# Taking a layer's experts in an order computed on the chip: most groups and fewest groups in turn

## The chip, the cores and the metric

One core of one Trainium2 chip runs one inference step of a two-layer network, all in float32. The metric is the time on the device in microseconds (us), lower is better. Three runs of the kernel before took 1150.02, 1155.69 and 1157.26 us.

## What is computed

There are 384 tokens of width 1024 (128 of the prompt, 256 of the sample). Layer 0 mixes tokens by a long convolution, layer 1 by attention; after each comes a mixture of experts, which is what the change touches:

```
g_sel  = argmax(t @ w_group + b_group)                 # one of 4 groups of experts
e_prob = softmax(of the 4 experts of that group)
top_w, top_i = top_k(e_prob, 2)                        # two experts of the 16 for each token
combine = sum over the two of one_hot(expert) * g_w * top_w
for e in range(16):
    a, b = split(t @ w_up[e], 2)
    y += combine[:, e] * ((silu(a) * b) @ w_down[e])
x = layer_norm(alpha * x + gate * y)
```

Each expert has 6 MB of weights: `w_up[e]` is 1024 x 1024 and `w_down[e]` 512 x 1024, float32. The sum over experts has no order of its own.

## The kernel before

**Groups.** The kernel computes an expert only for the tokens that chose it. A token's row is copied into one or two *slots*; an expert owns a whole number of groups of 32 slots (`SLOT_TOK`), at least one, and slots of expert 0 come first, then those of expert 1, and so on. With the inputs used there are 33 groups in each layer. For a group TensorE does three things in `expert(e, nb, base)`: 32 matmuls with the two up pieces, 12 matmuls that add the group before to the result (`combine`), 16 matmuls with the down piece. After an expert's last group a tiny matmul of the identity counts up `expert_done`.

**Weights.** They come in pieces of 2 MB, three to an expert: 48 pieces to a layer, numbered i = 3 * expert + c, c = 0 and 1 up, 2 down. The ring has 11 places (`RING + EXTRA`), so piece i goes where piece i - 11 was. SyncE (SP) issues the pieces in order, in `experts(l)`: an up place is free when `up_ready` has counted the last group of the expert that held it, a down place when `expert_done` has. Pieces 0 to 10 have conditions of their own, among them: piece 8 waits until VectorE has added `row_beta` to the last token tile (`ln_done`), piece 9 until the token rows have been written to their slots (`slots_filled`) and TensorE has gathered groups 0 to 2, piece 10 for `x_added`.

**Routing.** VectorE works out, in a chain of small operations in `moe(l)`, the groups of each expert (`nbase[:, 0:16]`), their running sum (`nbase[:, 16:32]`), each token's two slots (`pos`, then `idxf`), the integer slots (`idx_i`), and the integer counts `NBi`, which every engine reads into registers. `nb_ready` says that NBi is there, `idx_ready` and `idx_i_ready` the same of the slots. GpSimd (POOL) then writes the rows to DRAM in six scattered transfers. Groups 0 to 2 don't go by DRAM: VectorE makes one-hot matrices (`one_hot(n)`) and TensorE gathers these groups by matmul (`gather(n)`); `turned` transposes a gathered group for use. From group 3 on ScalarE loads rows from DRAM. `affine_b(2, row_beta[:])`, VectorE's work on the last token tile, stands between the write of NBi and `one_hot(1)`.

**After the experts.** Two last combining matmul rounds, a layer norm, and in layer 0 the loads for layer 1's attention, whose pieces use the same ring and follow in SP's queue.

Of the kernel before, what the change touches and what calls it, by code (L numbers as in the profile page):

```python
# [128 lines left out]
MC_ROW = MC_IOTA + SLOT_TOK  # L129
MC_COLS = MC_ROW + 1  # L130


def shape_constants():
# [30 lines left out]
    moe[:, MC_IOTA:MC_IOTA + SLOT_TOK] = np.arange(SLOT_TOK)  # L164
    moe[:, MC_ROW] = np.arange(128) % SLOT_TOK
    return {"k_dft": dft, "k_moe": moe, "k_zero": np.zeros((SLOT_TOK, D), np.float32)}, feat, cols

# [34 lines left out]
def build(nc, A, y_prompt, y_sample, new_k, new_v):  # L202
# [6 lines left out]
    with ctx:  # L209
# [73 lines left out]
        mc = at("mc", [128, MC_COLS], RM + 4416)  # L283
        nbase = at("nbase", [128, 33], RM + 2752)
        t96 = at("t96", [128, 2 * TT, 16], RM + 2912)
        NBi = at("NBi", [128, 33], RM + 3936, i32)
        idxf = at("idxf", [128, 2, TT], RM + 4096)
# [125 lines left out]
        def _(sp):  # L413
# [47 lines left out]
            def experts(l):  # L461
# [9 lines left out]
                def wait_used(i):  # L471
                    e, c = divmod(i, 3)
                    if c == 2:
                        sp.wait_ge(expert_done[l], e + 1)
                    else:
                        groups = sp.value_load(NBi[0:1, 17 + e:18 + e], min_val=1, max_val=MAX_BLOCKS)
                        sp.wait_ge(S["up_ready"], groups)

                for i in range(MOE_W):
                    e, c = divmod(i, 3)  # L480
                    if i == RING + EXTRA:
                        sp.wait_ge(nb_ready, l + 1)
                    if l == 1 and i == 4:
                        load_biases()
                    if i < RING:
                        wait_slot_free(first + i)
                    elif i == RING and l == 0:
                        for j in range(KT):
                            wait_evacuated(sp, G_AT["inv"] + j)
                    elif i == RING or i == RING + 1:  # L490
                        sp.wait_ge(group_ready, G_AT[f"out{l}_21"] + 1)
                        if l == 1:
                            sp.wait_ge(kv_out, 32)
                    elif i == RING + 2:
                        sp.wait_ge(group_ready, G_AT[f"tok{l}_2"] + 2)
                        sp.wait_ge(ln_done, TT * (2 * l + 1))
                    elif i == RING + 3:
                        sp.wait_ge(S["slots_filled"], 96)
                        sp.wait_ge(S["gathered"], 3)
                    elif i == RING + 4:  # L500
                        sp.wait_ge(S["x_added"], 1)
                    elif i >= RING + EXTRA:
                        wait_used(i - RING - EXTRA)
                    piece(first + i, up[e:e + 1, c * 512:(c + 1) * 512, :] if c < 2 else down[e:e + 1, :, :])

# [76 lines left out]
        def _(pool):  # L582
# [37 lines left out]
            def moe_side(l):  # L620
# [23 lines left out]
                pool.wait_ge(evacuated[G_AT[f"gf{l}"] % 8], G_AT[f"gf{l}"] // 8 + 1)  # L644
                total = whole_pairs(pool.value_load(NBi[0:1, 32:33], min_val=EXPERTS, max_val=MAX_BLOCKS))
                with pool.Fori(0, total - 1) as g:
# [33 lines left out]
        def _(pe):  # L680
# [219 lines left out]
            def moe(l):  # L900
# [104 lines left out]
                last.then_inc(spread_ready, 1)  # L1005
                pe.wait_ge(nb_ready, l + 1)
                nb, total = groups_of(0), 0
                pe.wait_ge(S["xgT_ready"], 1)
# [122 lines left out]
        def _(act):  # L1131
# [130 lines left out]
            def moe(l):  # L1262
# [41 lines left out]
                act.wait_ge(nb_ready, l + 1)  # L1304
                total = act.value_load(NBi[0:1, 32:33], min_val=EXPERTS, max_val=MAX_BLOCKS)
                gated(0)
# [90 lines left out]
        def _(dve):  # L1397
# [286 lines left out]
            def moe(l):  # L1684
# [17 lines left out]
                for k, oh in enumerate((o1, o2)):  # L1702
# [28 lines left out]
                wait_evacuated(dve, g)  # L1731
                link(v.tensor_copy(nbase[:, 32:33], t96[:, 0, 15:16]))
                link(v.tensor_tensor(t96[:].rearrange("p (k t) e -> p k (t e)", k=2), M12[:].rearrange("p (k t) e -> p k (t e)", k=2),
                                     pos[:].rearrange("p t e -> p (t e)").unsqueeze(1).to_broadcast([128, 2, 16 * TT]), ALU.mult))
# [35 lines left out]
                dve.wait_ge(spread_evac, 4 * (l + 1))  # L1770
                total = dve.value_load(NBi[0:1, 32:33], min_val=EXPERTS, max_val=MAX_BLOCKS)

# [171 lines left out]
```

## Time and profile before

| | us |
|---|---|
| median of three runs (1150.02, 1155.69, 1157.26) | 1155.69 |
| span of the profiled execution | 1154.0 |
| TensorE busy with matmuls in it | 1040.7 (90%) |
| VectorE busy | 600.8 (52%) |
| first group to last expert's end, layer 0 | 329.66 to 580.93 |
| first group to last expert's end, layer 1 | 871.81 to 1131.44 |

The profile records no time for that execution other than its span; the span lies between the lowest and the highest of the three runs. Moments are given in us from the start of the span. Busy time is that of an engine's records; a share of busy time of 90% doesn't say that TensorE is the bound in every stage, as it waits in some stages and not in others.

### The profile page before, as it was taken

How to read it: one execution, taken by the hardware profiler on the slowest of the kernel's cores; microseconds unless marked ns; L12 is line 12 of the kernel's file. 1: busy time of each engine (PE TensorE's matmuls, PEld its weight loads, DVE VectorE, ACT ScalarE, POOL GpSimd, SP SyncE). 2: the span in 40 equal slices, each digit the busy share in tenths (PEclk: the TensorE clock that was granted, in tenths of full speed). 3: DMA queues.
4: the chain of work that ended last, by engine and by line, in shares of the span. 5: the costliest groups of instructions: out<-in, count | busy, mean ns of one | idle time of the engine just before them, and what ended most of it. 6: DMA issues, size and time to landing. Idle time of an engine off the chain costs nothing.

```text
span 1154.0 us, 25964 instructions
## 1 busy us (share of the span) xinstructions
PE 1040.7 (90%) x10516; PEld 617.6 (54%) x10516; DVE 600.8 (52%) x1390; ACT 196.5 (17%) x479; POOL 172.1 (15%) x211
## 2 busy tenths in 40 slices
PE   5999998999897999999869899999989999677992
PEld 2555555375554665666545554575455666444661
DVE  5448999654632333333279991485563334122335
ACT  3231112002310100010040010362231010000002
POOL 1200000320030111122101000154012211101110
PEclk9999999999998999999979999799989999898997
DMA  9995567940789999994999978332089999999912
GB/s 339 402 327 197 192 243 290 370 134 1 290 307 390 389 390 390 389 368 167 390 397 336 391 275 328 119 101 82 8 321 337 388 387 390 395 398 397 389 53 98
DMA packets 114663, 333.39 MB, mean 289 GB/s; under 512 B 11649, under 2 KB 24385, under 8 KB 114209
## 3 DMA queue, kind: packets, MB, share of 16 engines
q1 hardware_dynamic: 91570, 299.65, 68.8%
q0 software_dynamic: 6224, 23.03, 5.9%
q10 hardware_dynamic: 16800, 9.72, 3.0%
q8 instruction: 52, 0.85, 0.3%
q14 instruction: 17, 0.14, 0.0%
HBM read 323.46 MB, written 20.45 MB: 298 GB/s over the span
## 4 chain that ended last, share of the span: by engine, by line
PE 68%; DMA 17%; DVE 8%; ACT 3%; issue 2%; POOL 1%; SPq 1%; another core or an unknown queue 0%; DVEq 0%; ACTq 0%
PE bank L688 67%; DMA ring<-in_moe_w_up 12%; DMA ring<-in_moe_w_down 2%; DMA ring<-in_na_w_qkv 2%; POOL P L670 1%; PE bank L1100 1%; ACT x L1239 1%; SPq L466 1%; DVE P L1868 1%; DVE hT L1625 1%; DVE st L1811 1%; DMA row_beta<-in_ln_b 1%; DVE ring L1444 1%; PE bank L861 0%; DVE x L1651 0%
## 5 line engine op out<-in xcount | busy, mean ns | idle before, releaser
L688 PE MATMUL bank<-ring,xgT 128*32 128x256 f32 x4224 | 254.0, 393 | 27.5 <-DMA ring<-in_moe_w_up 26.9
L688 PE MATMUL bank<-hT,ring 128*128 128x384 f32 x640 | 209.2, 489 | 7.6 <-DMA ring<-in_na_w_qkv 2.9
L688 PEld LDWEIGHTS bank<-ring,xgT 128*32 128x32 f32 x4224 | 146.8, 113 | 115.2 <-issue 25.2
L1776 DVE TENSOR_TENSOR he<-sa,bank 128x128 f32<-128x128 f32 x66 | 19.0, 288 | 339.0 <-ACT sa L1297 339.0
L688 PEld LDWEIGHTS bank<-hT,ring 128*128 128x128 f32 x640 | 122.1, 191 | 93.4 <-issue 7.1
L649 POOL TENSOR_TENSOR yg<-ysb,gate_s 128x256 f32<-128x256 f32 x128 | 91.0, 732 | 411.9 <-ACT ysb L1302 411.9
L1444 DVE CUSTOM_DVE_ANT_0 ring<-ring,ring 128x1024 f32<-128x1024 f32 x120 | 146.9, 1224 | 4.8 <-PE bank L688 1.0
L688 PE MATMUL bank<-ring,heT 128*32 128x256 f32 x2112 | 128.7, 384 | 10.9 <-DMA ring<-in_moe_w_down 10.9
L688 PE MATMUL bank<-yg,ohT 32*128 32x256 f32 x1632 | 110.4, 400 | 2.9 <-DVE yg L1805 2.9
L688 PEld LDWEIGHTS bank<-ring,heT 128*32 128x32 f32 x2112 | 63.4, 110 | 66.5 <-issue 33.6
L688 PEld LDWEIGHTS bank<-yg,ohT 32*128 32x128 f32 x1632 | 76.9, 190 | 37.9 <-issue 28.8
L1302 ACT ACTIVATE ysb<-bank 128x256 f32<-128x256 f32 x66 | 25.4, 384 | 226.4 <-PE bank L688 226.4
L1297 ACT ACTIVATE sa<-bank 128x128 f32<-128x128 f32 x66 | 18.3, 278 | 241.2 <-PE bank L688 241.2
L670 POOL TENSOR_SCALAR P<-P,den 128x384 f32<-128x384 f32 (+1 forms) x24 | 29.1, 1214 | 150.7 <-DVE den L1874 150.6
L688 PE MATMUL bank<-ring,yT 128*128 128x512 f32 x96 | 41.9, 593 | 1.1 <-DVE gate L1518 1.1
L688 PE MATMUL bank<-ring,qT 128*128 128x512 f32 x96 | 42.0, 593 | 0.8 <-DVE qT L1889 0.8
L1786 DVE SCALAR_TENSOR_TENSOR ohT<-pos_all,srow,wk_all 128x384 f32<-128x384 f32 x66 | 40.4, 612 | 2.2 <-PE bank L688 2.2
L688 PE MATMUL bank<-ring,hT 128*128 128x512 f32 x96 | 41.4, 592 | 0.0
L1789 DVE TENSOR_TENSOR ohT<-ohT,ohk 128x384 f32<-128x384 f32 x66 | 36.8, 558 | 2.3
L1783 DVE SCALAR_TENSOR_TENSOR ohk<-pos_all,srow,wk_all 128x384 f32<-128x384 f32 x66 | 38.0, 576 | 0.0
L1201 ACT ACTIVATE zt<-bank,first 128x128 f32<-128x128 f32 (+1 forms) x48 | 17.5, 419 | 110.1 <-PE bank L688 110.1
L688 PEld LDWEIGHTS bank<-ring,hT 128*128 128x128 f32 x96 | 18.2, 190 | 22.7 <-issue 22.5
(239 smaller groups left out, 1008.1 us busy)
## 6 DMA issues: line engine op xcount, KB each, us to landing
ring<-in_moe_w_up SPq DMA_DIRECT2D x64, 2048.0 KB, 25.3
ring<-in_moe_w_down SPq DMA_DIRECT2D x32, 2048.0 KB, 24.8
ring<-in_k_ada SPq DMA_DIRECT2D x15, 2048.0 KB, 15.9
ring<-in_w_ada SPq DMA_DIRECT2D x9, 2048.0 KB, 12.3
ring<-in_na_w_qkv SPq DMA_DIRECT2D x6, 2048.0 KB, 19.6
slots<-in_k_zero POOLq DMA_DIRECT2D x2, 5632.0 KB, 27.2
ring<-in_hy_w_in SPq DMA_DIRECT2D x5, 2048.0 KB, 12.2
group_row<-slots ACTq DMA_DIRECT2D x264, 32.0 KB, 5.2
```

Of the source, the lines that this page charges most:

```text
L466: sp.dma_start(w_view(i, 4, 1024), src.rearrange("o (k p) n -> p (o k) n", p=128)).then_inc(w_loaded[W_SLOT[i]], 16)
L649: nc.gpsimd.tensor_tensor(yg[:, c, :], ysb[:], gate_s[:, c, :], ALU.mult).then_inc(S["yg_ready"], 1)
L670: nc.gpsimd.tensor_scalar_mul(p, p, den[:, 2 * u:2 * u + 1]).then_inc(scaled[0], 1)
L688: return nc.tensor.matmul(out, lhsT, rhs, start=first, stop=last)
L1201: last = nc.scalar.activation(zt[:, n % 2, at_:at_ + b - a], ps[bank_of(g)][:, a:b], ACT.Identity, bias=VT[:, V_BIN + n:V_BIN + n + 1])
L1297: nc.scalar.activation(sa[:], ps[0][:, 0:128], ACT.Silu).then_inc(S["sa_ready"], 1)
L1302: nc.scalar.activation(ysb[:], ps[1][:, 0:256], ACT.Copy).then_inc(S["ysb_ready"], 1)
L1444: ins = v.tensor_tensor_reduce(scratch, w_view(i, 4, D)[:, q, :], cond_rows(l)[:, c * D:(c + 1) * D], 1.0, 0.0, ALU.mult, ALU.add, mod[l][ ...
L1776: v.tensor_tensor(he[:], sa[:], ps[0][:, 128:256], ALU.mult).then_inc(S["he_ready"], 1)
L1783: v.scalar_tensor_tensor(out=ohk[:], in0=pos_all[:, 0, :], scalar=srow[:], in1=wk_all[:, 0, :], op0=ALU.is_equal, op1=ALU.mult).then_inc(S ...
L1786: v.scalar_tensor_tensor(out=ohT[:].rearrange("p t n -> p (t n)"), in0=pos_all[:, 1, :], scalar=srow[:], in1=wk_all[:, 1, :], op0=ALU.is_e ...
L1789: v.tensor_tensor(ohT[:].rearrange("p t n -> p (t n)"), ohT[:].rearrange("p t n -> p (t n)"), ohk[:], ALU.add).then_inc(S["ohT_ready"], 1)
```

## The change

Experts 0 to 3 stay first, in their old order. The other twelve are ranked by their number of groups (key: 16 times the groups, minus the expert's number, so that of equals the lower number comes first), and taken as: the one with most, the one with fewest, the second most, the second fewest, and so on. VectorE works out this order, moves each expert's base and so each token's slots, and sorts group counts, running sums and expert numbers by the new order into `nbs`, which goes to `NBi` (49 columns, of 33 before). SP reads the number of the expert at each place from the fifth on into a register, once for three pieces, and takes the weights' address from it. The loop of TensorE, `expert(e, nb, base)`, is unchanged: e is now a place in the order. The diff (allocation of the new small tiles and the renamed columns of NBi cut):

```
@@ SP, experts(l)
-                        groups = sp.value_load(NBi[0:1, 17 + e:18 + e], min_val=1, max_val=MAX_BLOCKS)
+                        groups = sp.value_load(NBi[0:1, NB_CUM + 1 + e:NB_CUM + 2 + e], min_val=1, max_val=MAX_BLOCKS)
...
+                    if e < FIRST:
+                        who = slice(e, e + 1)
+                    elif c == 0:
+                        who = bass.ds(sp.value_load(NBi[0:1, NB_ID + e:NB_ID + e + 1], min_val=0, max_val=EXPERTS - 1), 1)
...
-                    piece(first + i, up[e:e + 1, c * 512:(c + 1) * 512, :] if c < 2 else down[e:e + 1, :, :])
+                    piece(first + i, up[who, c * 512:(c + 1) * 512, :] if c < 2 else down[who, :, :])
@@ TensorE, moe(l)
                 last.then_inc(spread_ready, 1)
-                pe.wait_ge(nb_ready, l + 1)
-                nb, total = groups_of(0), 0
                 pe.wait_ge(S["xgT_ready"], 1)
                 pe.wait_ge(S["oh_ready"], 2)
                 gather(1)
...
                 last.then_inc(S["x_added"], 1)
+                pe.wait_ge(nb_ready, l + 1)
+                nb, total = groups_of(0), 0
                 pe.wait_ge(S["ohT_ready"], 1)
@@ VectorE, moe(l)
-                link(v.tensor_copy(nbase[:, 32:33], t96[:, 0, 15:16]))
-                link(v.tensor_tensor(t96[:]..., M12[:]..., pos[:]..., ALU.mult))
-                v.tensor_reduce(idxf[:].rearrange("p k t -> p (k t)"), t96[:], AX, ALU.add).then_inc(idx_ready, 1)
-                dve.wait_ge(idx_ready, l + 1)
+                def picks():
+                    link(v.tensor_tensor(t96[:]..., M12[:]..., pos[:]..., ALU.mult))
+                    return v.tensor_reduce(idxf[:].rearrange("p k t -> p (k t)"), t96[:], AX, ALU.add)
+                link(picks())
...
-                v.tensor_copy(idx_i[:], idxf[:]).then_inc(S["idx_i_ready"], 1)
                 v.tensor_copy(rel[:], idxf[:].rearrange("p k t -> p (k t)")).then_inc(S["oh_moved"], 1)
                 one_hot(0)
-                v.tensor_copy(NBi[:], nbase[:]).then_inc(nb_ready, 1)
+                late = EXPERTS - FIRST
+                square = [128, EXPERTS, EXPERTS]
+                iota, order = mc[:, MC_IOTA:MC_IOTA + EXPERTS], mc[:, MC_ORDER:MC_ORDER + EXPERTS]
+                blocks = nbase[:, 0:16]
+                link(v.scalar_tensor_tensor(out=order_key[:], in0=blocks, scalar=float(EXPERTS), in1=iota, op0=ALU.mult, op1=ALU.subtract))
+                link(v.tensor_tensor(pairs[0][:, 0:late, 0:late], ..., ..., ALU.is_gt))
+                link(v.tensor_reduce(order_rank[:, FIRST:], pairs[0][:, 0:late, 0:late], AX, ALU.add))
+                link(v.tensor_scalar(order_rank[:, FIRST:], order_rank[:, FIRST:], 2.0, 0.5 - late, ALU.mult, ALU.add))
+                v.tensor_copy(order_at[:, 0:FIRST], order[:, 0:FIRST])
+                link(v.scalar_tensor_tensor(out=order_at[:, FIRST:], in0=order_rank[:, FIRST:], scalar=-1.0, in1=order_rank[:, FIRST:],
+                                            op0=ALU.mult, op1=ALU.min))
+                link(v.tensor_tensor(pairs[0][:], ..., ..., ALU.is_lt))
+                link(v.tensor_tensor(pairs[1][:], pairs[0][:], blocks.unsqueeze(1).to_broadcast(square), ALU.mult))
+                link(v.tensor_reduce(base_new[:], pairs[1][:], AX, ALU.add))
+                link(v.tensor_tensor(base_new[:], base_new[:], nbase[:, 16:32], ALU.subtract))
+                link(v.scalar_tensor_tensor(out=pos[:], in0=base_new[:]..., scalar=float(SLOT_TOK), in1=pos[:], op0=ALU.mult, op1=ALU.add))
+                picks().then_inc(idx_ready, 1)
+                dve.wait_ge(idx_ready, l + 1)
+                v.tensor_copy(idx_i[:], idxf[:]).then_inc(S["idx_i_ready"], 1)
+
+                link(v.tensor_tensor(pairs[0][:], ..., ..., ALU.is_equal))
+                for at_, what in ((0, blocks), (NB_ID, iota)):
+                    link(v.tensor_tensor(pairs[1][:], pairs[0][:], what.unsqueeze(1).to_broadcast(square), ALU.mult))
+                    link(v.tensor_reduce(nbs[:, at_:at_ + EXPERTS], pairs[1][:], AX, ALU.add))
+                link(v.tensor_tensor_scan(t96[:, 0, :], mc[:, MC_ONES:MC_ONES + 16], nbs[:, 0:16], 0.0, ALU.mult, ALU.add))
+                link(v.tensor_copy(nbs[:, NB_ALL:NB_ALL + 1], t96[:, 0, 15:16]))
+                link(v.tensor_tensor(nbs[:, NB_CUM:NB_CUM + EXPERTS], t96[:, 0, :], nbs[:, 0:16], ALU.subtract))
+                v.tensor_copy(NBi[:], nbs[:]).then_inc(nb_ready, 1)
                 v.tensor_copy(srow[:], mc[:, MC_ROW:MC_ROW + 1]).then_inc(S["srow_ready"], 1)
                 affine_b(2, row_beta[:])
```

`link` makes VectorE wait for its own last result before the next operation. Groups 0 to 2 lie in experts 0 to 3 whatever the order is, so that the gathering by one-hot matrices goes by the old slots.

## Rows read from the trace of the kernel before

**Rows 1.** The page: span, its DMA line, and groups of matmuls with their waits.

```profile
span 1154.0 us, 25964 instructions
...
DMA  9995567940789999994999978332089999999912
...
L688 PE MATMUL bank<-ring,xgT 128*32 128x256 f32 x4224 | 254.0, 393 | 27.5 <-DMA ring<-in_moe_w_up 26.9
...
L688 PE MATMUL bank<-ring,heT 128*32 128x256 f32 x2112 | 128.7, 384 | 10.9 <-DMA ring<-in_moe_w_down 10.9
```

**Rows 2.** The chain of waits in order: start us, us, what.

```profile
329.66 10.32 PE bank L688 x178
339.99 27.83 DMA ring<-in_moe_w_up
...
415.04 25.34 DMA ring<-in_moe_w_down
440.51 29.24 PE bank L688 x511
469.76 34.34 PE bank L688 x599
504.12 34.34 PE bank L688 x599
...
545.61 27.67 DMA ring<-in_moe_w_up
573.32 7.83 PE bank L688 x88
...
967.96 27.91 DMA ring<-in_moe_w_up
...
1037.09 25.59 DMA ring<-in_moe_w_up
```

**Rows 3.** Timeline of TensorE: start us, us, line, operation; [idle before it]; expert ends.

```profile
358.90 0.19 PE L688 MATMUL bank<-first 128*2 128x2 f32 x2
...
367.86 3.64 PE L688 MATMUL bank<-ring,xgT 128*32 128x256 f32 x32 [1.97 <-DMA ring<-in_moe_w_up]
...
1131.44 0.19 PE L688 MATMUL bank<-first 128*2 128x2 f32 x2
```

**Rows 4.** Stretches: us, engines' busy time (instructions), PE clock, DMA share, GB/s.

```profile
364.00:373.00 9.00, 7.03 (x68) 3.44 (x64) 1.09 (x4) 0.28 (x1) 0.00 (x0) 0.50 1.03 409
...
522.00:538.00 16.00, 16.00 (x288) 9.65 (x284) 7.43 (x21) 1.32 (x4) 2.84 (x4) 1.00 0.16 39
...
1000.00:1100.00 100.00, 83.28 (x1318) 50.52 (x1315) 28.38 (x77) 7.00 (x21) 15.61 (x22) 0.91 1.02 389
```

**Rows 5.** Timeline of VectorE in layer 0's routing.

```profile
308.52 0.17 DVE L1689 TENSOR_REDUCE mx<-Lg 128x3 f32<-128x12 f32 x1
308.72 0.17 DVE L1679 TENSOR_TENSOR sc<-Lg,mx 128x12 f32<-128x12 f32 x1
...
316.62 0.17 DVE L1752 CAST idx_i<-idxf 128x6 int32<-128x6 f32 x1
...
316.90 0.36 DVE L1741 TENSOR_TENSOR oh<-mc,rel 128x192 f32<-128x192 f32 x1
...
317.66 0.25 DVE L1755 CAST NBi<-nbase 128x33 int32<-128x33 f32 x1
...
319.54 0.25 DVE L1749 TENSOR_TENSOR hot<-oh 128x96 f32<-128x96 f32 x1
323.45 0.45 DVE L1761 STREAM_TRANSPOSE xgT<-bank 128x256 f32<-128x256 f32 x1 [3.67 <-remote]
```

**Rows 6.** VectorE's 256-element product, in the groups by shape: total us, mean ns.

```profile
L1805 DVE TENSOR_TENSOR yg<-ysb,gate_s 128x256 f32<-128x256 f32 x4 | 1.5, 422 | 2.2 <-ACT ysb L1302 2.2
```

**Rows 7.** Timeline of TensorE and VectorE around gather(1), both layers.

```profile
323.96 1.93 PE L688 MATMUL bank<-tok,hot 128*32 128x256 f32 x26 [1.23 <-DVE xgT L1761]
...
862.02 0.25 DVE L1749 TENSOR_TENSOR hot<-oh 128x96 f32<-128x96 f32 x1
...
865.78 2.23 PE L688 MATMUL bank<-tok,hot 128*32 128x256 f32 x33 [0.48 <-DVE xgT L1761]
```

**Rows 8.** Timeline of SP: start us, us, DMA issue.

```profile
319.19 0.37 SPq L466 DMA_DIRECT2D ring<-in_moe_w_down  x1
335.44 1.36 SPq L466 DMA_DIRECT2D ring<-in_moe_w_up  x2
```

**Rows 9.** Issues and register loads by line: median us or ns.

```profile
ring<-in_na_w_out SPq DMA_DIRECT2D x2, 2048.0 KB, 10.4
...
L476 SPq TENSOR_LOAD <-NBi x50: 262/274/477, 336.9 to 1075.4; - x50
...
L959 PEldq TENSOR_LOAD <-NBi x32: 296/301/682, 320.3 to 1089.1; - x32
...
L1292 ACTq DMA_DIRECT2D group_row<-slots x264: 318/322/1591, 340.3 to 1131.3; - x132
```

More of the change, by code:

```diff
@@ L129 @@
 MC_ROW = MC_IOTA + SLOT_TOK
-MC_COLS = MC_ROW + 1
+MC_ORDER = MC_ROW + 1
+MC_COLS = MC_ORDER + EXPERTS
+FIRST = 4
+NB_CUM, NB_ALL, NB_ID, NB_COLS = EXPERTS, 2 * EXPERTS, 2 * EXPERTS + 1, 3 * EXPERTS + 1
 def shape_constants():
@@ L165, in shape_constants @@
     moe[:, MC_ROW] = np.arange(128) % SLOT_TOK
+    moe[:, MC_ORDER:MC_ORDER + EXPERTS] = np.arange(EXPERTS) - (EXPERTS - 0.5)
     return {"k_dft": dft, "k_moe": moe, "k_zero": np.zeros((SLOT_TOK, D), np.float32)}, feat, cols
@@ L283, in build @@
         mc = at("mc", [128, MC_COLS], RM + 4416)
-        nbase = at("nbase", [128, 33], RM + 2752)
+        nbase = at("nbase", [128, 2 * EXPERTS], RM + 2752)
+        nbs = at("nbs", [128, NB_COLS], RM + 2176)
+        order_key, order_rank, order_at, base_new = (at(n, [128, EXPERTS], RM + 3520 + 64 * i)
+                                                     for i, n in enumerate(("order_key", "order_rank", "order_at", "base_new")))
+        pairs = [at("pairs0", [128, EXPERTS, EXPERTS], RM + 5888), at("pairs1", [128, EXPERTS, EXPERTS], RM + 9472)]
         t96 = at("t96", [128, 2 * TT, 16], RM + 2912)
-        NBi = at("NBi", [128, 33], RM + 3936, i32)
+        NBi = at("NBi", [128, NB_COLS], RM + 3296, i32)
         idxf = at("idxf", [128, 2, TT], RM + 4096)
@@ L644, in moe_side @@
                 pool.wait_ge(evacuated[G_AT[f"gf{l}"] % 8], G_AT[f"gf{l}"] // 8 + 1)
-                total = whole_pairs(pool.value_load(NBi[0:1, 32:33], min_val=EXPERTS, max_val=MAX_BLOCKS))
+                total = whole_pairs(pool.value_load(NBi[0:1, NB_ALL:NB_ALL + 1], min_val=EXPERTS, max_val=MAX_BLOCKS))
                 with pool.Fori(0, total - 1) as g:
@@ L1304, in moe @@
                 act.wait_ge(nb_ready, l + 1)
-                total = act.value_load(NBi[0:1, 32:33], min_val=EXPERTS, max_val=MAX_BLOCKS)
+                total = act.value_load(NBi[0:1, NB_ALL:NB_ALL + 1], min_val=EXPERTS, max_val=MAX_BLOCKS)
                 gated(0)
@@ L1731, in moe @@
                 wait_evacuated(dve, g)
-                link(v.tensor_copy(nbase[:, 32:33], t96[:, 0, 15:16]))
-                link(v.tensor_tensor(t96[:].rearrange("p (k t) e -> p k (t e)", k=2), M12[:].rearrange("p (k t) e -> p k (t e)", k=2),
-                                     pos[:].rearrange("p t e -> p (t e)").unsqueeze(1).to_broadcast([128, 2, 16 * TT]), ALU.mult))
-                v.tensor_reduce(idxf[:].rearrange("p k t -> p (k t)"), t96[:], AX, ALU.add).then_inc(idx_ready, 1)
-                dve.wait_ge(idx_ready, l + 1)
+                def picks():
+                    link(v.tensor_tensor(t96[:].rearrange("p (k t) e -> p k (t e)", k=2), M12[:].rearrange("p (k t) e -> p k (t e)", k=2),
+                                         pos[:].rearrange("p t e -> p (t e)").unsqueeze(1).to_broadcast([128, 2, 16 * TT]), ALU.mult))
+                    return v.tensor_reduce(idxf[:].rearrange("p k t -> p (k t)"), t96[:], AX, ALU.add)
+                link(picks())
                 def one_hot(n):
@@ new lines, in moe @@
+                blocks = nbase[:, 0:16]
+                link(v.scalar_tensor_tensor(out=order_key[:], in0=blocks, scalar=float(EXPERTS), in1=iota, op0=ALU.mult, op1=ALU.subtract))
+                link(v.tensor_tensor(pairs[0][:, 0:late, 0:late], order_key[:, FIRST:].unsqueeze(1).to_broadcast([128, late, late]),
+                                     order_key[:, FIRST:].unsqueeze(2).to_broadcast([128, late, late]), ALU.is_gt))
+                link(v.tensor_reduce(order_rank[:, FIRST:], pairs[0][:, 0:late, 0:late], AX, ALU.add))
@@ new lines, in moe @@
+                link(v.tensor_scalar(order_rank[:, FIRST:], order_rank[:, FIRST:], 2.0, 0.5 - late, ALU.mult, ALU.add))
+                v.tensor_copy(order_at[:, 0:FIRST], order[:, 0:FIRST])
+                link(v.scalar_tensor_tensor(out=order_at[:, FIRST:], in0=order_rank[:, FIRST:], scalar=-1.0, in1=order_rank[:, FIRST:],
+                                            op0=ALU.mult, op1=ALU.min))
+                link(v.tensor_tensor(pairs[0][:], order_at[:].unsqueeze(1).to_broadcast(square),
+                                     order_at[:].unsqueeze(2).to_broadcast(square), ALU.is_lt))
@@ new lines, in moe @@
+                link(v.tensor_tensor(pairs[1][:], pairs[0][:], blocks.unsqueeze(1).to_broadcast(square), ALU.mult))
+                link(v.tensor_reduce(base_new[:], pairs[1][:], AX, ALU.add))
+                link(v.tensor_tensor(base_new[:], base_new[:], nbase[:, 16:32], ALU.subtract))
+                link(v.scalar_tensor_tensor(out=pos[:], in0=base_new[:].unsqueeze(1).to_broadcast([128, TT, 16]),
+                                            scalar=float(SLOT_TOK), in1=pos[:], op0=ALU.mult, op1=ALU.add))
@@ new lines, in moe @@
+                picks().then_inc(idx_ready, 1)
+                dve.wait_ge(idx_ready, l + 1)
+                v.tensor_copy(idx_i[:], idxf[:]).then_inc(S["idx_i_ready"], 1)
+                link(v.tensor_tensor(pairs[0][:], order_at[:].unsqueeze(1).to_broadcast(square),
+                                     order.unsqueeze(2).to_broadcast(square), ALU.is_equal))
+                for at_, what in ((0, blocks), (NB_ID, iota)):
+                    link(v.tensor_tensor(pairs[1][:], pairs[0][:], what.unsqueeze(1).to_broadcast(square), ALU.mult))
+                    link(v.tensor_reduce(nbs[:, at_:at_ + EXPERTS], pairs[1][:], AX, ALU.add))
@@ L1770, in moe @@
                 dve.wait_ge(spread_evac, 4 * (l + 1))
-                total = dve.value_load(NBi[0:1, 32:33], min_val=EXPERTS, max_val=MAX_BLOCKS)
+                total = dve.value_load(NBi[0:1, NB_ALL:NB_ALL + 1], min_val=EXPERTS, max_val=MAX_BLOCKS)
                 def group(g, rows_sem, count, src):
```

## Prediction, made before the changed kernel ran

> **What bounds the kernel now.** I read the page first. TensorE is busy 90% of the span, and the DMA line stands at 9 for most of it [rows 1]: in the expert stages two resources run near full, and the question is which of them waits for the other. The groups of matmuls answer half of it: the up matmuls waited 26.9 us for weights, the down matmuls 10.9, 37.8 us in two layers. That is what a perfect order could give, before its own costs.
>
> The chain of waits shows the price of a group. Two pieces of it, 34.34 us each, run from one expert's end to the next with no wait [rows 2]. They are experts of five groups, so a group takes 34.34 / 5 = 6.87 us, and 33 groups take 226.7. The stages took 580.93 - 329.66 = 251.3 and 1131.44 - 871.81 = 259.6, so 24.6 and 32.9 us of them are waits and half-clock stretches around them.
>
> How many groups each expert has comes from TensorE's timeline: the tiny matmul after each expert (two of the 32 in [rows 3]) divides it, and each part is a multiple of 6.87 plus its waits. Layer 0: 1 1 1 1 3 3 1 2 5 5 5 1 1 1 1 1. Layer 1: 3 2 2 2 1 2 2 2 1 1 2 2 1 4 5 1.
>
> The weights' pace comes from the chain too. Pieces 13 and 26 of layer 0 landed at 339.99 + 27.83 = 367.8 and 415.04 + 25.34 = 440.4: 72.6 / 13 = 5.6 us for a piece. Pieces 28 and 40 of layer 1 landed at 995.9 and 1062.7: 5.6 again [rows 2]. An expert costs the DMA queues 3 x 5.6 = 16.8 us and TensorE 6.87 x groups: experts of one or two groups are bound by weights, those of three or more by TensorE. The ring holds under four experts. So a run of large experts fills it and stops the queue: from 522 to 538 the DMA share is 0.16 [rows 4]. A run of small ones empties it: there TensorE waits. In layer 1 the queue never stops from about 890 to 1100, and the large experts 13 and 14 stand at the end, when nearly all is loaded: 16 us of weights an expert come first, then 62 us of matmuls with an idle queue. This is what alternating mends.
>
> **The new order.** By the rule of the change the groups at places 0 to 15 are, in layer 0, 1 1 1 1 5 1 5 1 5 1 3 1 3 1 2 1, in layer 1, 3 2 2 2 5 1 4 1 2 1 2 1 2 1 2 2.
>
> **Cost before the first group: VectorE.** one_hot(0) ended at 317.6; without nbase's copy (0.2) and the old idx_i copy (0.1) ahead of it, it ends at 317.35. Then come, up to idx_i: four linked operations of 12 or 16 elements at 0.20 (such rows start 0.20 apart), an unlinked copy 0.1, two of 144 elements at 0.35, three of 256 at 0.46 (192 elements took 0.36 [rows 5], 256 took 0.42 [rows 6], plus 0.04 of linking), one of 48 at 0.24, two of 96 at 0.29. Sum 3.8: the idx_i copy starts at 321.15 instead of 316.62 [rows 5], 4.5 later. From there to NBi: that copy 0.2, five of 256, 2.3, and scan, copy and difference, 0.63: NBi's cast starts at 324.3 instead of 317.66 [rows 5], 6.7 later. Everything that VectorE has queued behind moves with it: srow, the addition of row_beta, one_hot(1), the transpose for group 0, one_hot(2).
>
> The three and five operations of 256 elements have no row of their own kind; the bounds are 0.35 (the 192-element row) and 0.55 each, so 6 to 7.6 us for the chain.
>
> The Trainium skill (VectorE: DVE Perf Modes, The TRN2 errata) gives 58 cycles plus the elements at 0.96 GHz, which would make 256 elements 0.33 us and this chain about 0.8 us shorter; by its own note that the formula under-predicts and the fixed part is near 150 cycles, 0.42. The trace agrees with the second [rows 5, 6].
>
> **What waits for it on TensorE.** gather(1) starts when the transpose is done. Before, that transpose waited at 323.45 for gather(0), 3.67 us after VectorE was ready [rows 5]: this hides part of the chain. New: one_hot(1) ends at 319.8 + 6.7 = 326.5, the transpose at 326.9, gather(1) starts at 327.0 instead of 323.96, 3.0 later. In layer 1 one_hot(1) ended at 862.3; 862.3 + 6.7 + 0.5 = 869.5 against 865.78 [rows 7]: 3.7 later. Then groups_of(0), which lay hidden in that wait, stands between x_added and the first group: its load took up to 0.68 us [rows 9], with its register operations 0.9. First groups: 4.0 later in layer 0 and 4.6 in layer 1. Bounds: 2.5 if the load hides behind the 2 us of x_added's matmuls and the chain is short, 7 if nothing hides.
>
> **What waits for it on the queues.** POOL's six scattered transfers wait for idx_i: 4.5 later. Piece 8, issued at 319.19 when row_beta was added [rows 8], is 6.7 later, but shares the queues with the scatter, so both are done about 4.5 later. Piece 9, at 335.44 for slots_filled [rows 8], moves by 4.5, and so does all that follows it while weights are the bound. Nothing hides this: the queue has nothing else. SP's own additions are one register load an expert, 0.27 us [rows 9] and some 0.2 of register operations; SP runs four to five pieces ahead of the landings (25 us from issue to landing [rows 2] against 5.6 a piece), which hides it; without that cover it would be 0.5 x 12 = 6 us a layer. An issue whose address comes from a register took ScalarE 0.32 us, as short as SP's 0.37 with a constant [rows 8, 9]: nothing.
>
> **Layer 0, summed.** Place 3 ends at 358.9 + 4.5 [rows 3], held by its pieces. Place 4 has to wait for piece 13, now at 367.8 + 4.5 = 372.3, and ends its first group 7.9 later as before, at 380.2 (half clock after the wait, below). 28 groups are left: 380.2 + 28 x 6.87 = 572.6, if no piece is late. I went through the places: piece i lands at 372.3 + (i - 13) x 5.65 and its place of the ring must be free some 3 us before its turn (a piece on an idle queue lands about 8.8 after its issue, 3 more than the 5.6 it occupies the queue). The tightest is piece 35: its ring place comes free when place 8's last up matmuls end, at 380.2 + 15 x 6.87 + 3.64 = 486.9, and its turn starts at 491. The last up piece, 46, lands at 559, place 15 wants it at 567. So the stage becomes bound by TensorE from place 4 on, and ends at 572.6: 8.3 us gained. The loads of layer 1's attention follow in the same queue, which no longer stands still from 522 to 538; their pieces were landing as TensorE's layer norm ran, so I take this gain to pass on whole.
>
> **Layer 1, summed.** 876.4 + 9 x 6.87 = 938.2 for place 4, whose five groups hold piece 12's place of the ring until 938.2 + 27.5 + 3.6 = 969.3. The queue has piece 22 landed at 995.9 - 6 x 5.6 + 4.6 = 966.9 and then runs dry: piece 23 is issued at 969.3 and lands some 8.8 later, 6 us after its turn (a pair issued on an idle queue took 10.4 in the middle, so the first about 8 [rows 9]). Piece 29 loses another 2 behind place 6. After that the places want weights faster than they come: 2 1 2 1 2 1 2 2 is 1.6 groups an expert, 11 us against 16.8. The last piece, 47, landed at 995.9 + 19 x 5.56 = 1101.5; now at 1101.5 + 4.6 + 8 = 1114.1. Then 1.9 for the down matmuls of the group and 6.87 for the second: 1122.9. Gained 8.5. After the stage nothing changes.
>
> Sum: 1154.0 - 8.3 - 8.5 = 1137.2 for the span. The median of the runs stands 1.7 above the span: 1138.9. Of the 37.8 us of waits the late start takes 9 and the part of layer 1 that stays bound by weights the rest.
>
> **The rivals.**
> (a) *The start is hidden.* If the chain's delay fell into existing slack, layer 0 would end at 568 and layer 1 at 1118: 27 us, 1129. For it speaks that the transpose waited 3.67; against, that piece 9 waits for the scatter with an idle queue. Chance 0.10.
> (b) *Half clock at the start.* With TensorE waiting longer ahead of gather(1), the clock may stand at 1.2 GHz for the gathers and the first group, as it stood at 0.50 right after the waits for weights around 363 [rows 4], where 32 up matmuls took 3.64 us [rows 3], twice what they take elsewhere. Before, it was full there. Each layer would start 1.8 to 3 later, in part hidden behind pieces: gain 12 to 15, 1142. The Trainium skill (TensorE: Matmul & The Clock Gate, Part 1: The HAM clock gate) has idleness throttle the clock and activity release it; by that rule the trace agrees, and this rival would come about. Chance 0.15.
> (c) *Weights slow down.* With no stretch of an idle queue in layer 0, and large experts spread among small ones, pieces run beside matmuls and row loads all the time. If a piece took 6.0 where it took 5.65, layer 0 would end near 579 and layer 1 near 1131: 1154, and 1147 for 5.85. Against it: 5.6 was measured under the same load, at a DMA share of 1.02 [rows 2, 4]. Chance 0.14.
> (d) *Slower: register-addressed issues limit the queue.* If an issue by SP with a computed address took longer than 5.6 us, the queue would run at SP's pace; that is the point from which it decides. At 6.2 us: 36 pieces x 0.6 x 2 = 43 us worse than the forecast, 1182. Against it stand ScalarE's 0.32 us. Chance 0.04.
> (e) *The order doesn't change*, or not as read: then only the late starts are left, 1155.7 + 9 = 1165. Chance 0.04.
>
> **How the numbers follow.** The forecast itself has 0.53, with 1133 to 1143 of its own (starts 2.5 to 7 us late, and the gap of layer 1 from 4 to 10). Predicted 1138.9. The range runs from (a), 1128, to the middle of (c), 1151; outside are (d), (e), half of (c) and bits of (a). About 1% (11.6 us) is what a measurement of this kernel tells from no change: faster than 1144 are the forecast, (a) and most of (b), 0.53 + 0.10 + 0.12, less some of the forecast's edge: 0.74. Slower than 1167 is (d) and a tail: 0.05. Same 0.21.
>
> **What the profile after would show.** TensorE's expert ends in the order of groups above; idx_i 4.5 and NBi 6.7 us later relative to one_hot(0), gather(1) 3 to 4 later; waits for weights on TensorE down from 38 to near 25 us, in layer 0 only at places 3 and 4, in layer 1 only from place 12 on; no stretch of idle queue in layer 0, one of 6 us near 969 less the layer 0 gain; the stages' ends 8 us and 17 us earlier. The forecast is wrong if pieces take over 5.8 us, if the ring stalls in layer 0 too, or if the first groups start over 7 us late.

## The result and the profile after

The changed kernel takes 1138.63 us, the median of four runs (1137.53 to 1140.54); its ratio to the kernel before is 0.984, 95% interval 0.982 to 0.986. A later comparison on another chip gave 1139.54 against 1156.78, 0.985 (0.983 to 0.987). One run of the kernel before that took 2150.23 us is left out of the first ratio.

The page of the changed kernel, the lines that answer to [rows 1]:

```profile
span 1138.7 us, 26215 instructions
...
DMA  9995467940669999999999979333077998999991
...
L700 PE MATMUL bank<-ring,xgT 128*32 128x256 f32 x4224 | 246.6, 385 | 12.2 <-DMA ring<-in_moe_w_up 11.7
...
L700 PE MATMUL bank<-ring,heT 128*32 128x256 f32 x2112 | 128.2, 383 | 11.6 <-DMA ring<-in_moe_w_down 11.6
```

The waits for weights fell from 37.8 us to 23.3. The DMA line has lost the 4 that marked the stopped queue of layer 0 (its 19th figure, 519 to 548 us); in layer 1 an 8 has come (the 34th figure, 939 to 968).

The chain of waits, in order (start us, us, what), against [rows 2]:

```profile
328.69 11.16 DMA slots<-tok,idx_i
...
351.13 25.94 DMA ring<-in_moe_w_down
377.20 77.35 PE bank L700 x1347
454.58 62.04 PE bank L700 x1077
...
861.58 0.46 DVE xgT L1807
862.08 155.22 PE bank L700 x2616
...
1083.19 24.47 DMA ring<-in_moe_w_down
...
1107.80 8.80 PE bank L700 x152
```

Layer 0 now has two parts. First the scatter sets the time (the rows written to the slots, which piece 9 waits for), then piece 14, the down piece that place 4 lacks; from 377.20 on TensorE runs to the stage's end without a wait. In layer 1 the chain stays on TensorE for 155 us and then goes over to SP's queue (those rows are not shown) and to the last piece, which lands at 1083.19 + 24.47 = 1107.7.

Stretches of the changed kernel: us, busy time of PE, PEld, DVE, ACT, POOL (instructions), PE clock, DMA share, GB/s; against [rows 4]:

```profile
325.00:332.00 7.00, 5.89 (x49) 2.67 (x50) 2.12 (x8) 0.77 (x2) 3.73 (x4) 0.52 0.94 303
500.00:545.00 45.00, 44.79 (x791) 27.72 (x786) 18.00 (x49) 4.36 (x13) 8.52 (x12) 1.00 1.03 391
955.00:985.00 30.00, 30.00 (x532) 18.66 (x528) 12.04 (x33) 2.93 (x9) 5.68 (x8) 1.00 0.82 297
```

From 500 to 545, where the queue had stopped, TensorE and DMA are both at full use. The stop of layer 1 is there, smaller: share 0.82 over 30 us near 970.

The start of layer 0 shows the price. VectorE, then TensorE (start us, us, operation [idle before]), against [rows 5, 7]:

```profile
316.44 0.25 DVE L1764 TENSOR_TENSOR hot<-oh 128x96 f32<-128x96 f32 x1
...
320.50 0.17 DVE L1791 CAST idx_i<-idxf 128x6 int32<-128x6 f32 x1
...
321.04 0.42 DVE L1796 TENSOR_TENSOR pairs<-pairs,nbase 128x256 f32<-128x256 f32 x1
...
323.56 0.33 DVE L1801 CAST NBi<-nbs 128x49 int32<-128x49 f32 x1
...
325.61 0.45 DVE L1807 STREAM_TRANSPOSE xgT<-bank 128x256 f32<-128x256 f32 x1
```

```profile
326.11 5.35 PE L700 MATMUL bank<-tok,hot 128*32 128x256 f32 x48 [3.98 <-DVE xgT L1807]
331.39 2.34 PE L700 MATMUL bank<-x,eye_alpha 128*128 128x512 f32 x4
333.66 2.58 PE L700 MATMUL bank<-ring,xgT 128*32 128x256 f32 x44
```

The transpose no longer waits; TensorE waits 3.98 us for it instead, and then does both gathers in 5.35 us. The clock column of the stretch 325 to 332 says why: 0.52, the 1.2 GHz level. Before, they took 3.8 (323.96 to 327.72, a gap of 0.3 in it, [rows 7] and the row below) at a granted clock of 1.00. That isn't their time at full clock either, which is 2.80 (filler and best, below); what made them longer before isn't known.

```profile
326.21 1.51 PE L688 MATMUL bank<-tok,hot 128*32 128x256 f32 x22 [0.32 <-issue]
```

The whole comes together when each stage is measured from one moment in the routing that the change leaves alone, VectorE's sum Msel, since what lies before it moves by a few us from run to run (309.6 to 314.2 in layer 0 over all kernels here). All from the profiled executions, in us from Msel:

| kernel | layer 0: first group | piece 9 lands | end | layer 1: first group | piece 9 lands | end |
|---|---|---|---|---|---|---|
| before | 16.9 | 31.0 | 268.2 | 16.5 | 30.9 | 276.1 |
| changed | 21.6 | 35.6 | 260.2 | 21.5 | 34.3 | 268.3 |
| changed, again | 19.8 | 35.2 | 259.7 | 20.2 | 35.7 | 269.0 |
| same_order | 19.9 | 35.4 | 271.8 | 21.1 | 35.5 | 281.0 |
| const_address | 20.1 | 34.6 | 272.0 | 20.1 | 35.7 | 282.3 |
| fewest_first | 20.0 | 35.0 | 268.6 | 20.4 | 36.6 | 262.6 |
| most_first | 20.0 | 34.9 | 278.4 | 20.4 | 36.2 | 270.5 |
| move_only | 17.4 | 30.1 | 267.9 | 16.5 | 29.5 | 275.9 |
| filler | 18.6 | 37.8 | 260.3 | 18.6 | 35.8 | 265.5 |
| first3 | 20.1 | 35.1 | 255.1 | 21.4 | 36.0 | 271.3 |
| split | 17.1 | 36.9 | 259.3 | 16.9 | 35.9 | 265.6 |
| best | 17.2 | 36.3 | 260.0 | 17.0 | 36.3 | 262.0 |
| known_order | 14.5 | 31.8 | 254.7 | 14.5 | 31.0 | 261.4 |

The two rows of the changed kernel agree within 0.7 at the ends, which tells how finely the column can be read. The part between the stages, from layer 0's end to layer 1's Msel, took 271.2 to 278.2 us in these executions; no edit touches it (but that known_order loads wider tables of constants), and it is why single times within 3 us say less than the table.

### The profile page after: what moved, and what is told of

Read it like the earlier page. It is cut to its first block, busy times and chain, and to the rows that moved or that the text cites. A ratio compares the mean times of both kernels' runs of the same rounds, so it can differ in the third digit from the quotient of the medians.

```text
span 1138.7 us, 26215 instructions
## 1 busy us (share of the span) xinstructions
PE 1038.1 (91%) x10516; PEld 616.2 (54%) x10516; DVE 612.3 (54%) x1430; ACT 197.1 (17%) x479; POOL 173.1 (15%) x211
## 4 chain that ended last, share of the span: by engine, by line
PE 70%; DVE 9%; DMA 8%; SPq 7%; ACT 3%; issue 2%; POOL 1%; DVEq 0%; POOLq 0%; ACTq 0%
PE bank L700 68%; SPq L474 6%; DMA ring<-in_moe_w_down 4%; DMA ring<-in_na_w_qkv 2%; PE bank L1112 1%; DMA slots<-tok,idx_i 1%; POOL P L682 1%; ACT x L1251 1%; DVE hT L1637 1%; DVE P L1914 1%; DVE st L1857 1%; DMA row_beta<-in_ln_b 1%; DVE ring L1456 1%; PE bank L873 0%; SPq L484 0%
## 5 line engine op out<-in xcount | busy, mean ns | idle before, releaser
L700 PE MATMUL bank<-ring,xgT 128*32 128x256 f32 x4224 | 246.6, 385 | 12.2 <-DMA ring<-in_moe_w_up 11.7
L700 PEld LDWEIGHTS bank<-ring,xgT 128*32 128x32 f32 x4224 | 144.4, 111 | 95.6 <-issue 13.3
L700 PEld LDWEIGHTS bank<-hT,ring 128*128 128x128 f32 x640 | 122.8, 192 | 92.9 <-issue 8.6
L700 PE MATMUL bank<-yg,ohT 32*128 32x256 f32 x1632 | 107.5, 392 | 3.0 <-DVE yg L1851 3.0
L700 PEld LDWEIGHTS bank<-yg,ohT 32*128 32x128 f32 x1632 | 74.7, 184 | 36.2 <-issue 27.6
L700 PEld LDWEIGHTS bank<-ring,hT 128*128 128x128 f32 x96 | 18.2, 190 | 22.7 <-issue 22.5
## 6 DMA issues: line engine op xcount, KB each, us to landing
ring<-in_moe_w_down SPq DMA_DIRECT2D x32, 2048.0 KB, 19.8
```

What stands on the lines that cost most here:

```text
L700: return nc.tensor.matmul(out, lhsT, rhs, start=first, stop=last)
```

## Experiments

**same_order: the price alone.** In the changed kernel:

```
-link(v.scalar_tensor_tensor(out=order_key[:], in0=blocks, scalar=float(EXPERTS), in1=iota, ...))
+link(v.scalar_tensor_tensor(out=order_key[:], in0=blocks, scalar=0.0, in1=iota, ...))
-link(v.tensor_scalar(order_rank[:, FIRST:], order_rank[:, FIRST:], 2.0, 0.5 - late, ...))
+link(v.tensor_scalar(order_rank[:, FIRST:], order_rank[:, FIRST:], 1.0, 0.5 - late, ...))
```

> The changed kernel with two constants changed so that the order worked out is the old one (all operations of the chain, the sorted NBi, the register addresses and the move on TensorE kept). My theory: the change is a gain of some 26 us by the order less a cost of some 9 by the late start. So this kernel pays the cost alone: first groups 4 to 5 us late in each layer, each stage's end 4 to 5 later than before, 8 to 10 us slower than before (about 1165). Rival, the start is hidden: no slower than before by over 2 us, and the order's whole worth is the 18 us seen.

1165.74 us, ratio to before 1.0085 (1.0059 to 1.0112), 8.1 us slower. The stages end 3.6 and 4.9 later than before. The chain has its old 34.34 pieces of five groups with no wait between, shifted by 4.5 ([rows 2]):

```profile
474.25 34.34 PE bank L700 x599
508.61 34.34 PE bank L700 x599
```

The price is real and, with the old order, as large as worked out; the rival falls. With the new order it's larger (known_order, below).

**const_address: without register addresses.** same_order with `who = slice(e, e + 1)` for all experts.

> same_order with the weights' addresses as constants again (SP reads no expert number): the whole chain, with the old order. Theory: register addresses cost nothing, as SP is four to five pieces ahead: the same as same_order, 1165, within 1.5 us. Rival: they cost up to 0.5 us for each late expert, 6 us a layer: 1153 to 1160.

1166.26 us, 1.0083 (1.0065 to 1.0101). Stages 272.0 and 282.3, against 271.8 and 281.0. Reading an expert's number and taking the address from it costs nothing that shows.

**known_order: the order without its price.** In the changed kernel the chain is cut out; bases and NBi are constants:

```
-v.scalar_tensor_tensor(out=pos[:], in0=nbase[:, 16:32].unsqueeze(1)...
+v.scalar_tensor_tensor(out=pos[:], in0=mc[:, MC_BASE:MC_BASE + 16].unsqueeze(1)...
...
+v.tensor_copy(NBi[:], mc[:, MC_NB:MC_NB + NB_COLS]).then_inc(nb_ready, 1)
```

It leaves out the working out of the order, takes the group counts as constants too, and holds for these inputs alone.

> The changed kernel without the chain that works out the order: the bases of the experts and the whole of NBi come as constants with the table k_moe, taken from the counts of these inputs (it holds for these inputs alone), and idx_i is written as early as in the kernel before. Order, register addresses and the move on TensorE are the changed kernel's. Theory: this is the order without its price. Piece 9 lands as in before (31 us after Msel, in the changed kernel 35), the first group starts 16.5 to 17.5 us after Msel (21.5), and the stages take about 255 and 262 us from Msel to the last expert's end (260.2 and 268.3): 9 to 11 us faster than the changed kernel, 1129. Rival: the price is no more than what split won (3 to 4 us), and the rest of the distance to the sum of the order is the order's own: 1135.

1126.50 us, 0.9735 (0.9712 to 0.9757): 30.3 us faster than before and 13.0 faster than the changed kernel on that chip. From Msel the stages are 13.5 and 14.7 us shorter than before. Against the changed kernel they are 5.5 and 6.9 shorter, against its repeat 5.0 and 7.6. The rival falls. The distance to the changed kernel, 13.0, is above the 9 to 11 expected: the stages give some 12.5 of it, and the part between them was the shortest of all in this profile (271.2).

**most_first and fewest_first: is it the alternating?**

```
-link(v.tensor_scalar(order_rank[:, FIRST:], order_rank[:, FIRST:], 2.0, 0.5 - late, ...))   # most_first
+link(v.tensor_scalar(order_rank[:, FIRST:], order_rank[:, FIRST:], 1.0, 0.5 - late, ...))
...
-order_key[:, FIRST:].unsqueeze(2).to_broadcast([128, late, late]), ALU.is_gt))              # fewest_first
+order_key[:, FIRST:].unsqueeze(2).to_broadcast([128, late, late]), ALU.is_lt))
```

> The changed kernel with one constant changed, so that the late twelve go by falling number of groups: layer 0 has 1 1 1 1 5 5 5 3 3 2 1 1 1 1 1 1, layer 1 has 3 2 2 2 5 4 2 2 2 2 2 2 1 1 1 1 1 1 cut to 16 places. My theory: three large ones in a row stop the queue again and the small ones at the end wait for weights: layer 0 some 20 us longer than in the changed kernel, layer 1 some 3 longer, about 1162. Rival, what gains is that large experts no longer stand at the end with all weights loaded: about 1139 or less.

1160.96 us, 1.0040 (1.0019 to 1.0061): slower than before. Layer 0 is 18.2 longer than in the changed kernel, layer 1 is 2.2 longer. (The list of layer 1 in the expectation is two too long; its places after the first six are 2 2 2 2 2 1 1 1 1 1.) Layer 0's pieces show both ends of it: the queue stops while the three large ones run (pieces 28 and 29 land 22 us apart), and the last places wait. TensorE's timeline of most_first:

```profile
559.82 3.64 PE L700 MATMUL bank<-ring,xgT 128*32 128x256 f32 x32 [3.72 <-DMA ring<-in_moe_w_up]
565.16 3.64 PE L700 MATMUL bank<-ring,xgT 128*32 128x256 f32 x32 [1.70 <-DMA ring<-in_moe_w_up]
...
576.01 3.46 PE L700 MATMUL bank<-ring,xgT 128*32 128x256 f32 x32 [3.71 <-DMA ring<-in_moe_w_up]
```

> The changed kernel with one comparison turned round, so that the late twelve go fewest, most, second fewest and so on: layer 0 has 1 1 1 1 1 5 1 5 1 5 1 3 1 3 1 2, layer 1 has 3 2 2 2 1 5 1 4 1 2 1 2 1 2 2 2. My theory of the ring (a piece each 5.6 us, place of the ring free after its last use) gives layer 0 some 10 us more than the changed kernel's, as a fifth small expert runs into missing weights, and layer 1 some 9 us less, as the queue is not stopped by a large expert when the ring is full: 1140, within 3 us of the changed kernel in total, but apart in each layer. Rival, it is the alternating as such that counts: each layer within 2 us of the changed kernel's.

1140.98 us, 0.9877 (0.9851 to 0.9903). Layer 0 is 8.5 longer than in the changed kernel (10 expected), layer 1 is 5.7 shorter (9 expected). The total alone would have been read as "no difference"; the stages say that two opposite effects cancel. Where the ring is empty, a fifth small expert costs 9 us of waiting: place 4 of layer 0 waits 9 us in both kernels, and with one group at place 4 instead of five, place 5 waits another 9.0. Where it is full, a large one stops the queue.

**first3: a large expert one place sooner.**

```
-FIRST = 4
+FIRST = 3
...
-                    if i == RING + EXTRA:
+                    if i == 3 * FIRST:
                         sp.wait_ge(nb_ready, l + 1)
```

> The changed kernel with three experts kept at the start instead of four (FIRST = 3; SP waits for NBi at piece 9 instead of 11). Layer 0: 1 1 1 5 1 5 1 5 1 3 1 3 1 2 1 1; layer 1: 3 2 2 5 1 4 1 2 1 2 1 2 1 2 1 2 or so. Theory of the ring: the wait of 9 us for piece 13 at place 4 of layer 0 goes, since a large expert now runs then: layer 0 about 6 us shorter; layer 1 stops the queue sooner and is 3 longer: 3 us faster than the changed kernel. Rival: the late start sets layer 0, no change.

1138.55 us, 0.9862 (0.9838 to 0.9887). Layer 0 is 5.1 shorter, layer 1 is 2.9 longer, near what was expected of each. The 3 us that it should have been faster by don't show: in the time it can't be told from the changed kernel.

**move_only: the edit on TensorE alone**, in the kernel before (wait for nb_ready and `groups_of(0)` behind x_added).

> The kernel before with one edit of the change: TensorE waits for nb_ready and reads the first count after x_added instead of ahead of gather(1). In the trace of before the signal of gather(0) came 3.7 us after its start (VectorE's transpose waited for it), in that of after 1.5. Theory 1, the register read between the matmuls holds up the signals of TensorE's matmuls: the signal comes some 2 us earlier, gather(1) too, and the first group 1 to 2 us earlier in both layers: 1 to 3 us faster than before. Theory 2, the scattered transfers running at the same time hold it up (they start just as early here): no change at the gathers, time as before within 1 us.

1158.13 us, 1.0014 (0.9999 to 1.0030). gather(0)'s signal comes 0.7 us sooner after its start than before, where theory 1 asked for some 2; VectorE of move_only:

```profile
324.12 0.45 DVE L1761 STREAM_TRANSPOSE xgT<-bank 128x256 f32<-128x256 f32 x1 [2.95 <-PE bank L688]
```

Theory 1 falls: neither the first groups nor the time gain. The move costs and gains nothing that shows in the time; the first group comes at 17.4 and 16.5, against 16.9 and 16.5 before. Theory 2, that the scatter holds the signal up, falls too: in known_order the scatter starts as early as here, and the signal comes 1.55 us after the start.

**filler: is it the clock?**

```
                 last.then_inc(spread_ready, 1)
+                for _ in range(15):
+                    mm(ps[0][:, 0:128], ident[:], ident[:])
                 pe.wait_ge(S["xgT_ready"], 1)
```

> The changed kernel with 15 spare 128x128 matmuls of the identity (into a part of bank 0 that the first group overwrites) between the spreading of idxf and the wait for the transpose, about 3.5 us of work in a wait of 4.0. Theory: the wait of 4 us ahead of gather(1) is what puts the clock to 1.2 GHz for both gathers (5.35 us in after, 3.4 in before); with TensorE busy they take 3.4 again and the first group comes 1.5 to 2 us earlier in each layer; layer 0 is held by piece 13 at place 4 and gives that back, layer 1 keeps it or loses it to the weights at its end: 0 to 2 us faster than the changed kernel. Rival: the gathers are slow for another reason (the scattered transfers), and stay at 5.35.

1140.59 us, 0.9879 (0.9857 to 0.9902). TensorE's timeline of filler:

```profile
319.73 3.51 PE L701 MATMUL bank<-first 128*128 128x128 f32 x30
323.81 2.80 PE L701 MATMUL bank<-tok,hot 128*32 128x256 f32 x48 [0.56 <-DVE xgT L1810]
```

The same 48 matmul records take 2.80 us at a granted clock of 1.00, against 5.35 in the first profile of the changed kernel and 4.05 and 4.38 in its repeat: the wait ahead of them, not the scatter that runs in both, set the clock down. The first group comes 3.0 and 2.9 sooner than in the first profile of the changed kernel, 1.3 and 1.6 sooner than in its repeat. Layer 0 gains nothing, as expected, held by its pieces (piece 9 was even later, 37.8); layer 1 is 2.8 to 3.5 shorter. In the whole time no gain shows.

**split: the chain cut in two.** The block that makes NBi, with a tile of its own for `pairs[0]`, moves behind the first uses:

```
                 v.tensor_copy(idx_i[:], idxf[:]).then_inc(S["idx_i_ready"], 1)
-                link(v.tensor_tensor(pairs[0][:], ..., ..., ALU.is_equal))
...
-                v.tensor_copy(NBi[:], nbs[:]).then_inc(nb_ready, 1)
                 v.tensor_copy(srow[:], mc[:, MC_ROW:MC_ROW + 1]).then_inc(S["srow_ready"], 1)
                 affine_b(2, row_beta[:])
                 one_hot(1)
                 dve.wait_ge(S["gathered"], 1)
                 turned(ps[1][:, 0:256])
                 one_hot(2)
                 dve.wait_ge(spread_ready, 2 * l + 2)
                 v.tensor_copy(pos_all[:, 0, :], ps[6][:, 0:TOK]).then_inc(spread_evac, 1)
+                link(v.tensor_tensor(pairs2[:], ..., ..., ALU.is_equal))
...
+                v.tensor_copy(NBi[:], nbs[:]).then_inc(nb_ready, 1)
```

> The changed kernel with VectorE's chain cut in two: as soon as the slots are there (idx_i), the addition of row_beta, one_hot(1), the transpose, one_hot(2) and the copy of pos_all go first, and what is needed for NBi alone after them (in a tile of its own). Theory: gather(1) starts about 3 us sooner and at full clock, piece 8 is issued 3 sooner, NBi is there when TensorE wants it: first groups 4 to 5 us sooner than in the changed kernel; layer 0 gains only what the scatter and piece 9 gain (0 to 1), layer 1 gains 1 to 4 at its stopped queue: 2 to 5 us faster than the changed kernel. Rival: nb_ready becomes the bound in place of gather(1): nothing.

1136.82 us, 0.9837 (0.9815 to 0.9859). The first groups come 4.5 and 4.6 sooner than in the changed kernel; layer 0 gains 0.9, layer 1 2.7, in sum 3.6. The ratio can't be told from the changed kernel's 0.984 and 0.985, so the 2 to 5 us expected of the time aren't shown.

**best: split, first3 and fewest_first together.**

> split, first3 and fewest_first together: layer 0 has 1 1 1 1 5 1 5 1 5 1 3 1 3 1 2 1, as in the changed kernel, layer 1 has 3 2 2 1 5 1 4 1 2 1 2 1 2 2 2 2 or so. Theory of the ring: layer 0 as in split, layer 1 about 7 us shorter than the changed kernel's: 8 to 11 us faster than the changed kernel in all, about 1129. Rival: layer 1 is bound by the last piece whatever the order (weights from the first to the last without a stop), then no more than 6 faster in layer 1's stage.

1132.19 us, 0.9803 (0.9783 to 0.9823). Expected were 8 to 11 us less than the changed kernel, about 1129; by the ratios it is some 4 to 6, so this was missed.

> The kernel called best (cut chain, three experts kept first, fewest first) again, beside the changed kernel on this chip: 6 to 8 us faster than it, by the stages layer 1 alone.

1132.98 us, 0.9797 (0.9776 to 0.9818).

**change_again: the changed kernel beside it.**

> The changed kernel itself, to stand beside the others on this chip: 0.984 of before.

1139.54 us, 0.9852 (0.9833 to 0.9870), on the same chip as best_again, which is 6.6 us faster. The stages of best are 260.0 and 262.0 (best_again's lie within 0.3 of them), so layer 1 alone gains, 6.3 (7.0 against the repeat), near the 7 expected. The rival (bound by the last piece, 6 at most) isn't told apart by the size, and its picture is what the trace of best shows: in layer 1 pieces 12 to 47 land 5.7 us apart in the mean, at most 7.2, and the stage ends 8.8 us after the last one.

TensorE's timeline of best: the gathers at full clock, and a short wait left ahead of the first group, now for its count in NBi (the profile names no releaser; NBi's cast starts at 324.58, after the copy of pos_all):

```profile
320.62 2.80 PE L701 MATMUL bank<-tok,hot 128*32 128x256 f32 x48 [0.91 <-DVE xgT L1798]
323.35 1.98 PE L701 MATMUL bank<-x,eye_alpha 128*128 128x512 f32 x4
326.88 3.44 PE L701 MATMUL bank<-ring,xgT 128*32 128x256 f32 x60 [1.55 <-issue]
```

## Why the prediction was right

**The price of a group and the pace of a piece.** 6.87 us and 5.6 us held in every kernel; 34.34 for five groups came again in same_order. Both stages could be worked out from them, and so could other orders: of the eight stages of most_first, fewest_first, first3 and known_order, the lengths lie within 2 us of what the expectations said, but for fewest_first's layer 1 (3.3 off).

**VectorE's chain.** Forecast 3.80 us from one_hot(0) to idx_i and 3.15 on to NBi; it was 320.50 - 316.69 = 3.81, and 3.06. The operations of 256 elements took 0.42, as the neighbouring row had said ([rows 6]).

**The late start.** Forecast 4.0 and 4.6 us, measured 4.7 and 5.0 in the first profile (2.9 and 3.7 in the repeat). Two of its terms were off and nearly cancelled, which is luck: gather(1) came about when forecast (2.8 and 3.6 later, forecast 3.0 and 3.7), but groups_of(0) cost nothing instead of 0.9, as it hides behind x_added (which ends at 331.39 + 2.34 = 333.7, when the first group starts), and the half clock of rival (b), which the forecast left out, came: the gathers took 1.6 and 1.2 us longer than before, x_added 0.3 to 0.4. I had given that 0.15; filler shows its mechanism. In layer 0 it cost nothing, for the reason that the rival named, the pieces; in layer 1 filler's stage is 2.8 to 3.5 shorter, so there it did cost.

**The queues.** Piece 9 was forecast 4.5 later and was 4.7 and 3.3 (4.2 and 4.8 in the repeat). same_order shows that the late start costs 8.5 us over the stages where the order is the old one, const_address that the addresses are no part of it.

**Layer 0.** Forecast gain 8.3; from Msel it was 8.0 (8.5 in the repeat). The wait at place 4 stood where it was put, and no other after it. The queue didn't stop.

**Layer 1.** Forecast gain 8.5; 7.8 (7.1 in the repeat). Piece 23 landed 11.9 us after piece 22, 6.3 over its turn, where 6 was forecast. The other 2 us forecast at piece 29 aren't there, it came 5.8 us after piece 28; piece 24, right behind the stop, took 6.8. The last piece landed at 1107.7. From place 12 on TensorE waits for weights, as said.

**The sum.** 16.8 forecast, 15.8 in the stages and 15.3 in the span, so the stages' gain passed on, less what the part between them varies by. That the median fell within 0.3 us of the forecast is partly luck: that part alone varies by several us.

**The rivals.** (a) falls by same_order. Its size, 27 us for a free order, was about right: known_order has 28.2 in its stages, though its first groups come 2.4 and 2.0 us sooner than the kernel before's, which isn't the order's doing. (c) falls: 5.6 to 5.7 us a piece in the stretches without a stop. (d) falls by const_address, (e) by the counts of groups at the expert ends, which are those listed.

**The price in layer 1.** It grows from 4.9 (same_order) to 6.9 to 7.6 (changed against known_order), and the traces tell why. Piece 23 goes where piece 12 was, and piece 12 is an up piece of place 4, whose five groups hold it until 13 groups and the up matmuls of one more are done, 13 x 6.87 + 3.6 = 92.9 us from the first group on. So TensorE's start sets when piece 23 is issued. First group (TensorE) and issue of piece 23 (SP), in the changed kernel and in known_order:

```profile
869.59 2.78 PE L700 MATMUL bank<-ring,xgT 128*32 128x256 f32 x46
962.40 0.37 SPq L474 DMA_DIRECT2D ring<-in_moe_w_down  x1
...
854.26 3.66 PE L711 MATMUL bank<-ring,xgT 128*32 128x256 f32 x64
947.08 0.37 SPq L485 DMA_DIRECT2D ring<-in_moe_w_down  x1
```

It is 92.8 us in both, and again in the repeat, filler and split, whose first groups come at 20.2, 18.6 and 16.9. With the old order place 4 has one group and frees the piece's place long before its turn (70.4 us after the first group SP begins the issue), so there layer 1 pays only for the late piece 9. known_order's first group is 7.0 us sooner than the changed kernel's, and the last piece lands 6.9 sooner. The repeat's stage ends 1.7 us later behind its last piece than the others: the final 9 us have a mean granted clock of 0.83 there, of 1.00 in the changed kernel's first profile and in known_order.

## What to carry to other kernels

When two resources are near full in turns, work out each item's need of both, and place items so that neither the buffer runs full nor empty: here TensorE takes 6.87 us a group, the queue 16.8 an expert, and the ring holds under four. It isn't alternating that gains but meeting the buffer's state: the same rule, started from the other end, was 8.5 us worse in one layer and 5.7 better in the other. An order worked out on the chip is paid at the start, where the queue has nothing else to do: the stages of the changed kernel are 15.8 us shorter than before, those of known_order 28.2. Putting first what the next transfers and gathers need, and only then what names the order, made the stages of split 3.6 us shorter; in the time that isn't clear of the noise.

## What the runs showed of the hardware

With a wait of 3.7 to 4.0 us ahead of the gathers, TensorE's granted clock fell to its 1.2 GHz level, and 15 spare matmuls (30 records) in the gap kept it at 2.4 GHz (filler: 2.80 us for the gathers, granted clock 1.00). Waits of 0.5 to 1.2 us there (before, split, best) left it at 1.00. The Trainium skill (TensorE: Matmul & The Clock Gate, Part 1: The HAM clock gate) has idleness throttle the clock and activity release it, and the trace agrees.

What the wait costs varies. The gathers took 5.35 us at a mean granted clock of 0.50 in both layers of the first profile, 4.05 and 4.38 at 0.68 and 0.63 in the repeat, after waits of the same 3.9 to 4.0 us; the first groups came 1.3 to 1.7 us sooner for it.

In the kernel before, gather(0)'s signal came 3.7 us (layer 0) and 2.9 us (layer 1) after its start at a granted clock of 1.00, in move_only 2.9 and 2.2; in the profiles of all other kernels here 1.55, in both layers. The two kernels with the late signals also took 3.8 to 4.7 us for gather(1) and gather(2) at a granted clock of 1.00, known_order 2.80. Neither the register read on TensorE (move_only) nor the scatter explains it, as known_order has the scatter as early as move_only. What does stays open.
